# A condition's shift sums moved from VectorE to TensorE in the front of a decoder block, Trainium2, one core

## What is computed

```python
mod = jax.nn.silu(c) @ ada_w[l] + ada_b[l]
shift1, scale1, gate1, shift2, scale2, gate2 = jnp.split(mod[:, None, :], 6, axis=-1)
g = norm_gains[l]
h = rms_norm(x, g[0]) * (1.0 + scale1) + shift1
y = hybrid_mixer(h, positions, w_in[l], ...)      # begins with proj = h @ w_in
x = x + gate1 * rms_norm(y, g[1])
h = rms_norm(x, g[2]) * (1.0 + scale2) + shift2
y = peer_ffn(h, ...)                              # 512 x 128 rows gathered from two tables of experts
```

## Time and profile before

| | us |
|---|---|
| median of 3 runs | 4460.79 (4457.4 to 4464.49) |
| the profiled execution, its own time | 4471.04 |
| its span, first to last instruction | 4469.0 |
| PE busy | 2835.3 (63%) |
| DVE busy | 2218.7 (50%) |
| POOL busy | 1674.9 (37%) |
| ACT busy | 541.4 (12%) |
| DMA, mean rate | 316 GB/s |

### The profile page before, as it was taken

How to read it: one execution, slowest core, us unless ns; L and a number is a source line. 1 busy time by engine, 2 the same in 40 slices (tenths; PEclk the granted TensorE clock), 3 DMA queues, 4 the chain that set the end, 5 groups by cost and what they waited for, 6 DMA issues and landing times.

```text
span 4469.0 us, 37335 instructions
## 1 busy us (share of the span) xinstructions
PE 2835.3 (63%) x15012; PEld 1638.2 (37%) x15012; DVE 2218.7 (50%) x3468; ACT 541.4 (12%) x1191; POOL 1674.9 (37%) x1160
## 2 busy tenths in 40 slices
PE   3777879766789999999697334344433334444445
PEld 2665768656787545545354011011011011001000
DVE  7335373575417533232556455665466664444442
ACT  2211212120011000101211000110001101001000
POOL 2465253411000323323223345644455554444342
PEclk9888989887889999999898555555555555555555
DMA  7411222189855889898787989999999999999998
GB/s 289 172 68 66 76 75 86 59 333 380 340 199 186 348 320 361 329 356 338 284 331 273 422 351 403 412 412 422 422 396 414 415 411 422 421 422 421 421 422 371
DMA packets 291434, 1413.20 MB, mean 316 GB/s; under 512 B 24384, under 2 KB 24512, under 8 KB 150720
## 3 DMA queue, kind: packets, MB, share of 16 engines
q0 software_dynamic: 156672, 1140.92, 62.3%
q1 hardware_dynamic: 128672, 257.97, 16.4%
q10 hardware_dynamic: 5920, 11.94, 0.7%
HBM read 1403.35 MB, written 7.39 MB: 316 GB/s over the span
## 4 chain that ended last, share of the span: by engine, by line
PE 41%; DMA 36%; DVE 10%; POOL 8%; issue 3%; ACT 2%; SPq 0%; ACTq 0%; POOLq 0%; DVEq 0%
PE psum L559 41%; DMA front<-in_down,back 23%; DMA front<-in_up,back 8%; POOL front L530 4%; POOL w_low L509 3%; DMA front<-in_w_in 3%; DVE front L1459 3%; DVE back L1220 1%; DMA back<-in_ada_w 1%; ACT back L1046 1%; POOL back L530 0%; DVE back L1437 0%; DMA front<-in_w_conv_o 0%; DVE back L1403 0%; DVE back L1394 0%
## 5 line engine op out<-in xcount | busy, mean ns | idle before, releaser
L559 PE MATMUL psum<-front 128*32 128x512 f32 (+2 forms) x6608 | 1425.7, 667 | 1032.8 <-DMA front<-in_up,back 850.0
L1459 DVE CUSTOM_DVE_ANT_0 front<-front,back 128x2048 f32<-128x2048 f32 x512 | 1169.3, 2292 | 1394.0 <-DMA front<-in_down,back 1270.2
L559 PEld LDWEIGHTS psum<-front 128*32 128x32 f32 (+1 forms) x6608 | 597.8, 166 | 1792.5 <-issue 1409.4
L530 POOL DMA_INDIRECT front<-in_down,back x512 | 625.4, 1221 | 900.1 <-DVE back L1459 658.8
L530 POOL DMA_INDIRECT front<-in_up,back x442 | 535.1, 1211 | 1004.7 <-PE psum L559 956.6
L559 PE MATMUL psum<-back,front 128*32 128x128 f32 (+3 forms) x4400 | 638.6, 456 | 345.2 <-DMA back<-in_up,back 163.2
L559 PEld LDWEIGHTS psum<-back,front 128*32 128x32 f32 (+1 forms) x4400 | 374.9, 168 | 617.9 <-issue 332.9
L509 POOL TENSOR_TENSOR w_low<-front,w_high 128x2048 fp32r<-128x2048 f32 x52 | 370.7, 7132 | 452.7 <-ACT w_high L934 452.7
L559 PE MATMUL psum<-x_high,w_high 128*128 128x512 f32 x640 | 260.1, 406 | 137.1 <-POOL w_low L509 114.3
L559 PE MATMUL psum<-x_low,w_high 128*128 128x512 f32 x640 | 257.5, 402 | 0.0
L559 PE MATMUL psum<-x_high,w_low 128*128 128x512 f32 x640 | 256.8, 401 | 0.0
(11 more groups left out here) (156 smaller groups left out, 1627.1 us busy)
## 6 DMA issues: line engine op xcount, KB each, us to landing
front<-in_w_in SPq DMA_DIRECT2D x116, 1024.0 KB, 4.9
front<-in_ada_w POOLq DMA_DIRECT2D x64, 1024.0 KB, 10.2
back<-in_ada_w SPq DMA_DIRECT2D x32, 1024.0 KB, 7.6
front<-in_w_out SPq DMA_DIRECT2D x32, 1024.0 KB
front<-in_w_q SPq DMA_DIRECT2D x32, 1024.0 KB
front<-in_w_conv_o SPq DMA_DIRECT2D x16, 1024.0 KB
front<-in_w_attn_o SPq DMA_DIRECT2D x16, 512.0 KB
front<-in_down,back POOLq DMA_INDIRECT x512
```

The costliest lines, as they stand in the source:

```text
L530: nc.gpsimd.indirect_dma_start(out=row_, out_offset=None, in_=table[:, :], in_offset=bass.IndirectOffsetOnAxis(ap=idx4[:, t % 2, c:c + 1], ...
L559: return nc.tensor.matmul(o, a, b, start=start, stop=stop)
L1459: V.tensor_tensor_reduce(d_row[s], d_row[s], h2r, 1.0, 0.0, ALU.mult, ALU.add, pre[:, b // 16 % 2, b % 16:b % 16 + 1]).then_inc(dots_done, 1)
```

## The change

The shift's half of the sums goes to PE. A new function `shift_rows(q, i)` multiplies the four tiles kk of a shift load by their silu columns, each repeated 32 times, so that tile kk's sums over its 128 rows land in 32 equal rows of bank 3, at partitions 32kk to 32kk + 31. In quarter 0 the four calls stand at the start of PE's program; in later quarters one stands ahead of each transposed tile, all of them behind the product of the quarter before. DVE keeps the scale's 16 instructions a quarter and gains one: it copies bank 3, divided by 32, into `first_sum[1]`, from where `columns` adds it up as before. SP's wait ahead of a shift load is now for PE's count (`ada_summed`), ahead of a scale load for DVE's.

```diff
@@ ada_load (SP)
                         if n >= 4:
-                            sp.wait_ge(ada_used, n - 3)
+                            sp.wait_ge((ada_used, ada_summed)[j], n // 2 - 1)
@@ PE
+            def shift_rows(q, i):
+                n = 8 * q + 2 * i + 1
+                pe.wait_ge(ada_in[n % 4], 16 * (n // 4 + 1))
+                if q and i == 0:
+                    pe.wait_ge(ab_ready, q)
+                for kk in range(4):
+                    ins = mm(ps[32 * kk:32 * kk + 32, 3, :], csil[:, 4 * i + kk:4 * i + kk + 1].to_broadcast([P, 32]),
+                             first_ada[n % 4][:, kk, :], i == 0, i == 3)
+                ins.then_inc(ada_summed, 1)
+
+            pe.wait_ge(csil_ready, 1)
+            for i in range(4):
+                shift_rows(0, i)
             pe.wait_ge(xn_ready, TT)
             for q in range(4):
                 for k in range(4 * q, 4 * q + 3):
+                    if q:
+                        shift_rows(q, k - 4 * q)
                     transpose_x(k)
-                pe.wait_ge(ada_used, 8 * (q + 1))
                 if q:
-                    pe.wait_ge(ab_ready, q)
+                    shift_rows(q, 3)
+                pe.wait_ge(ada_used, 4 * (q + 1))
+                pe.wait_ge(shift_copied, q + 1)
@@ DVE
             for q in range(4):
                 for i in range(4):
+                    n = 8 * q + 2 * i
+                    dve.wait_ge(ada_in[n % 4], 16 * (n // 4 + 1))
                     for kk in range(4):
-                        for j in range(2):
...
+                        total, part = first_sum[0], first_ada[n % 4][:, kk, :]
+                        weight = csil[:, 4 * i + kk:4 * i + kk + 1]
+                        if i == 0 and kk == 0:
+                            ins = V.tensor_scalar(total, part, weight, None, ALU.mult)
+                        else:
                             if kk == 0:
+                                dve.wait_ge(ada_used, n // 2)
                             else:
+                                st.seen(st.n)
+                            ins = V.scalar_tensor_tensor(total, part, weight, total, ALU.mult, ALU.add)
...
                 if q == 0:
                     normalise()
+                dve.wait_ge(ada_summed, 4 * (q + 1))
+                V.tensor_scalar(first_sum[1], ps[:, 3, :], 1.0 / 32, None, ALU.mult).then_inc(shift_copied, 1)
                 dve.wait_ge(modT_done, q + 1)
```

More of the change, by code:

```diff
@@ L313, in block_kernel @@
         ada_used = sem("ada_used")
+        ada_summed = sem("ada_summed")
+        shift_copied = sem("shift_copied")
         ada2_in = [sem(f"ada2_in{s}") for s in range(4)]
@@ L1205, in _ @@
                 for i in range(4):
+                    n = 8 * q + 2 * i
+                    dve.wait_ge(ada_in[n % 4], 16 * (n // 4 + 1))
                     for kk in range(4):
-                        for j in range(2):
-                            n = 8 * q + 2 * i + j
-                            total, part = first_sum[j], first_ada[n % 4][:, kk, :]
-                            weight = csil[:, 4 * i + kk:4 * i + kk + 1]
+                        total, part = first_sum[0], first_ada[n % 4][:, kk, :]
[3 more added lines that the diff above has]
+                        else:
                             if kk == 0:
-                                dve.wait_ge(ada_in[n % 4], 16 * (n // 4 + 1))
-                            if i == 0 and kk == 0:
-                                ins = V.tensor_scalar(total, part, weight, None, ALU.mult)
-                            else:
[L1216 to L1224, removed]
+                                dve.wait_ge(ada_used, n // 2)
+                            else:
+                                st.seen(st.n)
+                            ins = V.scalar_tensor_tensor(total, part, weight, total, ALU.mult, ALU.add)
+                        if kk < 3:
+                            st.did(ins)
+                        else:
+                            ins.then_inc(ada_used, 1)
                 if q == 0:
                     normalise()
+                dve.wait_ge(ada_summed, 4 * (q + 1))
+                V.tensor_scalar(first_sum[1], ps[:, 3, :], 1.0 / 32, None, ALU.mult).then_inc(shift_copied, 1)
                 dve.wait_ge(modT_done, q + 1)
```

## The result

The changed kernel takes 4488.34 us, the median of 4 runs (4485.81 to 4488.45), against 4460.26 for the kernel before in the same comparison: ratio 1.0061, 95% interval 1.0043 to 1.0078, or 28 us slower. The forecast was 4484.6, slower. The profiled execution took 4488.42.

What follows compares the result with a forecast made beforehand. The prediction took the front to be bound by DVE's sums and loads, with PE's product hidden beside them. 4460.8 plus 23.8 (the front's last product ending at 199.8 against 176.1) gave 4484.6 us, range 4472 to 4494.

Steps and rivals of the forecast that it cites:

- 23.8 us of loss in the front: End of the front's last product, 199.8 against 176.1: quarter 0's gain less the longer periods of quarters 1 to 3.
- Quarter 0: First quarter: shorter DVE sums and a normalisation ahead of `w_low` bring colA at 50.9 instead of 61.5, gaining 10.6.
- The ring stalls at the product: Quarters 1 to 3: load 8q + 5 waits for PE's product; third load lands at T + 11.2, weights T + 13.9.
- T: The end of the product of the quarter before, from which the steps of quarters 1 to 3 are counted.
- Behind the load: Quarters 1 to 3: last `shift_rows` 1.1, copy 0.7 and `columns` 3.1 follow the third load, to T + 16.1.
- ColA held by w_low: Quarters 1 to 3: `w_low` runs from T + 15.9 to T + 20.4 and holds L1231; colA and colB at T + 20.6.
- Periods: Quarters 1 to 3: a period of 42.7 in place of 31.0, with 8.3 and 13.8 behind colA as now.
- Switching shapes: PE: a change of tiling mode drains TensorE, and each `shift_rows` changes it twice; charged nothing.
- the rival without a hold: ColA at T + 15.3, ahead of `w_low`; POOL's `x_low` sets a period of 39.8: 16.0 later, 4476.8. Chance 0.30.
- No change: The front's delay is taken up again by waits of POOL and DVE behind it: 4461. Chance 0.06.
- Faster by a ring that never stalls: Loads land under the product if PE reaches two `shift_rows` before it; periods of 27.5, 20.6 sooner, 4440. Chance 0.07.
- The serial products: The four products of a `shift_rows` do not run beside one another: 4.3 each, not 1.1; 4504. Chance 0.05.

Runs made afterwards that it cites:

- run with `w_low` put behind: Kernel before the change, with one GpSimd wait added so quarter 0's `w_low` runs behind the normalisation: 4460.15 against 4461.76, ratio 0.9996.
- runs with one and with two `shift_rows` ahead: Changed kernel with one or two of the next quarter's `shift_rows` ahead of the product: 4471.78 (ratio 1.0021) and 4446.37 (ratio 0.9962).
- weights-first run: Changed kernel with the projection weights' load issued ahead of load 8q + 4 in quarters 1 to 3: 4478.28, ratio 1.0035 to the kernel before.
- doubled run: Changed kernel with every product of `shift_rows` made twice and the copy's factor halved to 1/64: 4492.40, ratio 1.0071 to the kernel before.
- two-ahead run: Changed kernel with the next quarter's first two `shift_rows` ahead of the product instead of behind it: 4446.37 against 4462.31, ratio 0.9962.

## Why the prediction was right

The forecast of 4484.6 lies 3.7 below the measured median, its 23.8 us of loss in the front (199.8 less 176.1 is 23.7) against 24.7 measured, and the chain is the one it wrote down. The other 3.4 of the 28.1 measured come from no step of it, and no run explains them. By its steps:

- **Quarter 0.** ColA at 50.9 forecast, 51.4 measured. All four normalisations went ahead of `w_low` (39.83 + 4.89 = 44.7, POOL's instruction begins at 44.01 but ends 0.6 late, at 49.09, held in its turn). The run with `w_low` put behind shows that 4.1 of the gain are that hold.
- **The ring stalls at the product.** Right in place: 2 GB/s under the product, SP's first load at T + 1.1, 8.97 for the third load behind it (forecast 9.4, from T + 1.8 to T + 11.2). The runs with one and with two `shift_rows` ahead show it as cause, by removing a part and then all of it.
- **Behind the load.** Two terms were too small, and only one of them was swallowed by the hold. A `shift_rows` has 8 matmul records, not 4: an f32 product of this shape leaves two. So it takes 1.06 at clock 1.0 and 1.93 at 0.5, twice what I took from the earlier trace rows, where I read eight records as eight products, and they were four. The first `shift_rows` stands ahead of the loads, so its 0.5 counts in full: the third load landed at T + 11.7, `w_low` ended at T + 20.9, both 0.5 behind the forecast. The last one took 1.11, 1.98 and 1.11, where I had 1.1: right in two quarters by luck, with half of the cost at half of the clock that it had. `columns` took 3.56 at a granted clock of 0.50, not 3.1 (the row of 3.10 was at 0.59). Bank 3 was ready at T + 17.3 in quarter 1 and T + 18.1 in quarter 2, not T + 16.1, and the hold hid what of this lay behind the loads.
- **ColA held by w_low.** Right; forecast T + 20.6, measured 94.6, or T + 21.1 with the product's end at 73.5. The weights-first run shows the hold as cause, and that it is worth 7.3 in all. (The 7.8 between the forecast and the rival without a hold is no test of this: there GpSimd's `x_low` behind `w_low` set the period, here `w_low` is over during the product.) The doubled run shows that work between the loads and the hold is free. The order itself was close: forecast 0.4 apart, measured 1.1 (`w_low` from 89.91, L1251 at 90.98), and 0.3 in the doubled run.
- **Periods.** 43.2, 42.2 and 43.1 from colA to colA (51.4, 94.6, 136.9, 180.0) against 42.7.
- **Switching shapes.** I charged nothing for it, and none shows: the first `shift_rows` began at 73.51, where the product's last instruction is modelled to end at 73.58, and the transposes at 74.51, within its 1.06.
- **The rivals.** Faster by a ring that never stalls needed the order that the two-ahead run makes, and there it came out at a period of 27.9, where the rival said 27.5. The serial products are out: eight records ended in 1.06. No change is out by the interval.

A rule bears on the hold of L1251. The Trainium skill's GPSIMD Engine Reference, Specifications, says that GpSimd shares its SBUF interfaces with VectorE, and that instructions of VectorE in a 2-port mode or with two SBUF inputs contend. The trace agrees for L1251: it has two SBUF inputs and was held, and L1250, which reads PSUM and SBUF, took 0.17 while `w_low` ran. The normalisation (one input, f32, 1.28 for 2048 elements) was held too; that it runs in a 2-port mode, which the rule asks for, no view shows. For DMA three loads in a row can be set against the estimate by the Trainium skill's DMA: Bandwidth & Descriptors (Anatomy of one DMA), 9.2 from the first issue of three. The Trainium skill gives this figure for DMAs issued by GpSimd, and these are SyncE's. The first was issued right behind the first `shift_rows`, at 74.64, and the third landed at 85.2: 10.6, 1.4 more than the estimate.

## What to carry to other kernels

When work moves from one engine to another, its buffers are freed by the new engine in the new engine's order: look for the longest instruction run ahead of it there, and ask which load waits for that. Moving the freeing calls ahead of the long run, with no work saved, turned a loss of 28 us into a gain of 16. And a step that looks added to a serial chain may be free, or saving it worthless, when another branch (here the weights through GpSimd) holds the joint behind it; a step ahead of the point where that branch starts counts in full.

## What the runs showed that I had not expected

- The granted clock in the profile is not always the speed of the products. In the changed kernel, 28 to 32 us has 1.00 in the clock's column, yet the `shift_rows` in it took 1.94, as the one from 127.47 did at 0.50 (1.93); behind the first product, it took 1.06. In the first product itself, with 1.00 in the column, the first instructions start 0.43 apart and those from 65.7 on 0.23. The window, then the two calls in the timeline of PE:

```profile
28.00:32.00 4.00, 1.94 (x8) 0.20 (x8) 1.62 (x4) 2.60 (x4) 0.00 (x0) 1.00 1.05 387
```

```profile
28.48 1.94 PE L561 MATMUL psum<-back 128*32 128x512 f32 x8 [8.12 <-DMA back<-in_ada_w]
...
73.51 1.06 PE L561 MATMUL psum<-back 128*32 128x512 f32 x8
```

- With the products of `shift_rows` doubled, the granted clock was 1.00 during the `columns` behind them in two quarters of three (1.93 each), and 0.50 in the third (3.56); without, it was 0.50 in all three (3.56). Why the one quarter differed is open.
- A hold works both ways. GpSimd's `w_low` of quarter 0, started at 44.01 with the last normalisation still running, took 5.08 in place of 4.5:

```profile
44.01 5.08 POOL L511 TENSOR_TENSOR w_low<-front,w_high 128x2048 fp32r<-128x2048 f32 x1 [43.55 <-ACT w_high L954]
```
